# Low halves of the weights: subtraction moved from GpSimd to VectorE, and the order of TensorE's passes

## The reference

```python
for l in range(DEPTH):
    shift, scale, gate = split(silu(c) @ w_ada[l] + b_ada[l], 3)
    proj = (x * (1 + scale) + shift) @ w_in[l]
    y_a = a_b * causal_dwconv(a_c * a_x, conv_a[l]) * silu(a_g)      # width 3
    y_b = dilated_attention(q, k, v, rel_bias) * silu(b_g)           # 8 heads of 64
    y_c = rglru(c_x) * silu(c_g)        # conv of width 4, gates, linear recurrence
    y_d = s5(d_u) * silu(d_g)           # complex diagonal recurrence, gelu, GLU
    y = concatenate([y_a, y_b, y_c, y_d]) @ w_out[l]
    x = layer_norm(ALPHA * x + (1 + gate) * y, ln_g[l], ln_b[l])
```

## Time and profile before

| | |
|---|---|
| Time, median of 3 runs | 2152.26 us (2152.07 to 2152.48) |
| Profiled execution: its span (no other time of it is given) | 2154.4 us |
| Busy: PE, DVE, ACT, POOL | 1850.3, 1515.3, 546.3, 683.6 us |
| Splits on POOL | 256, 629.8 us, mean 2461 ns |
| TensorE clock granted, mean | 0.908 of full speed |

### The profile page before, as it was taken

How to read it: one execution, slowest core, us unless ns; L and a number is a source line. 1 busy time by engine, 2 the same in 40 slices (tenths; PEclk the granted TensorE clock), 3 DMA queues, 4 the chain that set the end, 5 groups by cost and what they waited for, 6 DMA issues and landing times.

```text
span 2154.4 us, 24427 instructions
## 1 busy us (share of the span) xinstructions
PE 1850.3 (86%) x7335; PEld 1366.0 (63%) x7335; DVE 1515.3 (70%) x2383; ACT 546.3 (25%) x796; POOL 683.6 (32%) x341
## 2 busy tenths in 40 slices
PE   2229898899899989969997989998999998979994
PEld 1117566667666766656885756775776775757883
DVE  5787897799789869972324588578668839852755
ACT  2103222322222223222112322322332222232111
POOL 2115232323332232322443523332332333223441
PEclk9558898999899989979998889999998999989997
DMA  7786225524642552353333423421342342234432
GB/s 269 246 288 181 78 80 178 162 82 132 184 126 79 175 161 87 112 161 128 97 98 127 121 74 103 123 90 59 103 130 67 99 121 83 71 100 149 164 98 88
DMA packets 294715, 273.25 MB, mean 127 GB/s; under 512 B 23928, under 2 KB 220896, under 8 KB 291560
## 3 DMA queue, kind: packets, MB, share of 16 engines
q1 hardware_dynamic: 294632, 272.36, 40.3%
HBM read 261.81 MB, written 10.51 MB: 126 GB/s over the span
## 4 chain that ended last, share of the span: by engine, by line
PE 43%; DVE 41%; issue 6%; DMA 6%; SPq 3%; POOL 1%; DVEq 1%; ACT 0%; POOLq 0%
DVE work L1126 13%; PE bank L728 12%; PE bank L729 12%; PE bank L730 12%; DVE ada_acc L1134 7%; DMA ada_in<-in_w_ada 4%; DVE work L1006 3%; DVE work L1005 2%; DVE work L1134 2%; DVE work L1130 2%; DVE y_t L1134 2%; PE bank L869 1%; DVE carry L1134 1%; PE bank L756 1%; DVE carry L1126 1%
## 5 line engine op out<-in xcount | busy, mean ns | idle before, releaser
L484 POOL TENSOR_TENSOR w_lo<-raw,w_hi 128x1024 fp32r<-128x1024 f32 x256 | 629.8, 2461 | 1274.0 <-ACT w_hi L536 1274.0
L728 PE MATMUL bank<-op_hi,w_hi 128*128 128x512 f32 x1536 | 639.8, 417 | 5.1 <-POOL w_lo L484 5.1
L729 PE MATMUL bank<-op_lo,w_hi 128*128 128x512 f32 x1536 | 618.9, 403 | 0.0
L730 PE MATMUL bank<-op_hi,w_lo 128*128 128x512 f32 x1536 | 616.7, 401 | 0.0
L536 ACT ACTIVATE w_hi<-raw 128x1024 fp32r<-128x1024 f32 x256 | 270.8, 1058 | 1178.7 <-PE bank L730 1129.4
L728 PEld LDWEIGHTS bank<-op_hi,w_hi 128*128 128x128 f32 x1536 | 302.6, 197 | 122.6 <-issue 53.2
L730 PEld LDWEIGHTS bank<-op_hi,w_lo 128*128 128x128 f32 x1536 | 300.5, 196 | 67.6
L729 PEld LDWEIGHTS bank<-op_lo,w_hi 128*128 128x128 f32 x1536 | 301.9, 197 | 61.5 <-issue 1.9
L1134 DVE SCALAR_TENSOR_TENSOR ada_acc<-ada_in,cond,ada_acc 128x512 f32<-128x512 f32 (+1 forms) x256 | 258.1, 1008 | 50.8 <-DMA ada_in<-in_w_ada 33.4
L728 PE MATMUL bank<-w_hi,op_hi 128*128 128x512 f32 x512 | 200.0, 391 | 0.0
L729 PE MATMUL bank<-w_lo,op_hi 128*128 128x512 f32 x512 | 199.2, 389 | 0.0
(11 more groups left out here) (188 smaller groups left out, 1747.3 us busy)
## 6 DMA issues: line engine op xcount, KB each, us to landing
raw<-in_w_in SPq DMA_DIRECT2D x192, 512.0 KB, 4.0
ada_in<-in_w_ada SPq DMA_DIRECT2D x256, 256.0 KB, 3.8
raw<-in_w_out SPq DMA_DIRECT2D x64, 512.0 KB, 3.7
raw<-in_w_ada SPq DMA_DIRECT2D x24, 512.0 KB, 5.1
ada_in<-in_w_ada SPq DMA_DIRECT2D x16, 512.0 KB, 5.7
bias_t<-in_w_ada SPq DMA_DIRECT2D x8, 512.0 KB, 5.1
work<-in_w_ada SPq DMA_DIRECT2D x8, 512.0 KB, 6.0
rot<-in_w_ada SPq DMA_DIRECT2D x8, 512.0 KB, 6.1
```

The lines of the kernel that those rows point to most:

```text
L484: pool.tensor_tensor(w_lo[:, n % NHL, :], raw[:, n % NRAW, :], w_hi[:, n % NHL, :].bitcast(F32), ALU.subtract).then_inc(s.lo_done.sem, 1)
L728: pe.matmul(out_, xh, wh, start=first, stop=False)
L729: pe.matmul(out_, xh, wl, start=False, stop=False)
L730: return pe.matmul(out_, xl, wh, start=False, stop=last)
```

## The change

The split of the low halves leaves POOL (L484). `split_lo` becomes a function of DVE, with the same waits, and is called at fixed places of DVE's program (`lo(...)`). PE's piece is taken apart: it waits for hi(n) alone, runs the 16 matmuls that use the weights' high half, waits for lo(n), and runs the other 8. The output stage keeps its order of matmuls. The 15 (layer 0) or 4 ada pieces in one call are divided by lo(21) in layer 0. SP's and ACT's programs are unchanged.

```diff
--- before.py
+++ after.py
@@ -475,31 +475,10 @@
 
 
             for l, s in enumerate(layers):
-                pool.sem_inc(s.lo_done.sem, NRAW)
-                def split_lo(n, step, ahead=0):
-
-                    pool.wait_ge(s.hi_done.sem, s.hi_done.at(n + 1, step) + ahead * HALF)
-
-                    pool.wait_ge(s.mm_done.sem, s.mm_done.at(n + 1 - NHL, step) + ahead * HALF)
-                    pool.tensor_tensor(w_lo[:, n % NHL, :], raw[:, n % NRAW, :],
-                                       w_hi[:, n % NHL, :].bitcast(F32), ALU.subtract).then_inc(s.lo_done.sem, 1)
-
                 for k in range(KT):
-                    if k == FIRST_SPLIT[l]:
-                        split_lo(0, 0)
-                        split_lo(1, 0)
                     pool.wait_ge(s.op_hi.sem, k + 1)
                     pool.tensor_tensor(op_lo[:, k, :], hf[:, k % 2, :], op_hi[:, k, :].bitcast(F32),
                                        ALU.subtract).then_inc(s.op_lo.sem, 1)
-
-
-                with pool.Fori(0, CT) as ct:
-                    for n in range(2, HALF):
-                        split_lo(n, ct)
-                    split_lo(0, ct, 1)
-                    split_lo(1, ct, 1)
-                for n in range(2, W_OUT):
-                    split_lo(n, CT)
 
 
         @block.scalar
@@ -849,14 +828,19 @@
                         u, half = n // 2, n % 2
                         if half == 0:
                             is_free(u % 2, u // 2)
+                        pe.wait_ge(s.hi_done.sem, s.hi_done.at(n + 1, ct))
+                        for j in range(KH):
+                            k, w = half * KH + j, slice(P * j, P * (j + 1))
+                            if u == 0:
+                                pe.wait_ge(s.op_lo.sem, k + 1)
+                            pe.matmul(bank[u % 2][:, :], w_hi[:, n % NHL, w], op_hi[:, k, :], start=k == 0, stop=False)
+                            pe.matmul(bank[u % 2][:, :], w_hi[:, n % NHL, w], op_lo[:, k, :], start=False, stop=False)
+
                         pe.wait_ge(s.lo_done.sem, s.lo_done.at(n + 1, ct))
                         for j in range(KH):
-                            k = half * KH + j
-                            if u == 0:
-                                pe.wait_ge(s.op_lo.sem, k + 1)
-                            w = slice(P * j, P * (j + 1))
-                            mm = product(bank[u % 2][:, :], (w_hi[:, n % NHL, w], w_lo[:, n % NHL, w]),
-                                         (op_hi[:, k, :], op_lo[:, k, :]), k == 0, k == KT - 1)
+                            k, w = half * KH + j, slice(P * j, P * (j + 1))
+                            mm = pe.matmul(bank[u % 2][:, :], w_lo[:, n % NHL, w], op_hi[:, k, :],
+                                           start=False, stop=k == KT - 1)
                         mm.then_inc(s.mm_done.sem, 1)
                         for part in between[n]:
                             part()
@@ -882,6 +866,7 @@
                     c, kk = n // 8, n % 8
                     if n == 8:
                         pe.wait_ge(s.gb.sem, 4)
+                    pe.wait_ge(s.hi_done.sem, s.hi_done.at(n + 1, CT))
                     pe.wait_ge(s.lo_done.sem, s.lo_done.at(n + 1, CT))
                     for t in range(ST):
                         if c >= 2 and kk == 0:
@@ -897,6 +882,13 @@
                             mm.then_inc(s.y_mm.sem, 1)
                     mm.then_inc(s.mm_done.sem, 1)
 
+        def split_lo(dve, s, n, step, ahead=0):
+
+            dve.wait_ge(s.hi_done.sem, s.hi_done.at(n + 1, step) + ahead * HALF)
+            dve.wait_ge(s.mm_done.sem, s.mm_done.at(n + 1 - NHL, step) + ahead * HALF)
+            dve.tensor_tensor(w_lo[:, n % NHL, :], raw[:, n % NRAW, :], w_hi[:, n % NHL, :].bitcast(F32),
+                              ALU.subtract).then_inc(s.lo_done.sem, 1)
+
         def branch_loop(dve, l, s, line, own, tt, ts, stt, repeat):
 
             ADD, SUB, MUL = ALU.add, ALU.subtract, ALU.mult
@@ -909,6 +901,10 @@
                 for b, before in ((1, 5), (4, 1), (5, 1), (6, 1), (7, 1)):
                     s.free[b].local = before
                 pieces = [0]
+
+                def lo(*ns):
+                    for n in ns:
+                        split_lo(dve, s, n, ct)
 
                 def ada(*counts):
 
@@ -950,6 +946,7 @@
                 own(ts(rot[:, 1, :, :], turns, ROUND, ADD, ROUND, SUB), s.own)
                 own(tt(turns, turns, rot[:, 1, :, :], SUB), s.own)
                 own(stt(rot[:, 1, :, :], turns, -1.0, turns, MUL, ALU.max), s.to_act)
+                lo(2)
                 ada(4, 1)
                 for i in range(2):
                     for g in range(2):
@@ -970,7 +967,9 @@
                             own(op_, s.bb_done)
                         else:
                             own(op_, s.own)
+                lo(3)
                 ada(4, 1)
+                lo(4, 5)
 
 
                 unit_copied(dve, s, "c_x", ct)
@@ -979,8 +978,9 @@
                     own(stt(xc, xp[:, k:k + S], col("conv_c", 4 * k), xc, MUL, ADD), s.own)
                 own(stt(xc, xp[:, 0:S], col("conv_c"), xc, MUL, ADD), s.xc_done)
                 ada(4, 2)
-
-                def s5_tile(q):
+                lo(6)
+
+                def s5_tile(q, *splits):
                     cos = rot[:, 1, q, :].unsqueeze(1).to_broadcast([P, 4, TC])
                     sin = rot[:, 0, q, :].unsqueeze(1).to_broadcast([P, 4, TC])
                     w_re, w_im, t_, x_re, x_im = (v.rearrange("p (a b) -> p a b", a=4) for v in s5_s)
@@ -1010,6 +1010,8 @@
                             own(tt(carry[:, 2:3], e_im, cl, MUL), s.own)
                             own(stt(carry[:, 1:2], e_re, cl, carry[:, 0:1], MUL, SUB), s.own)
                             own(stt(carry[:, 3:4], e_re, sl, carry[:, 2:3], MUL, ADD), s.own)
+                        if c == 1:
+                            lo(*splits)
 
                     dve.wait_ge(s.c_done.sem, s.c_done.at(q, ct))
                     own(tt(x_re, w_re, cos, MUL), s.own)
@@ -1044,34 +1046,43 @@
                     unit_copied(dve, s, use_name, ct)
                     return stt(dst, gt[:, i, :], 1.0, gx[:, i, :], ADD, MUL)
 
-                s5_tile(0)
-
+                lo(7)
+                s5_tile(0, 8)
+                lo(9)
 
                 dve.wait_ge(s.from_act.sem, s.from_act.at(2, ct))
                 own(ts(lru_s[0], lru_s[0], 1.0, ADD), s.own)
                 own(dve.reciprocal(lru_s[0], lru_s[0]), s.own)
                 own(tt(lru_s[2], lru_s[2], lru_s[0], MUL), s.own)
+                lo(10)
                 own(ts(lru_s[0], lru_s[0], 2.0, MUL, -1.0, ADD), s.own)
                 own(stt(lru_s[1], lru_s[1], 1.0, xc, ADD, MUL), s.own)
                 own(tt(lru_s[1], lru_s[1], lru_s[2], MUL), s.own)
                 own(dve.tensor_tensor_scan(xc, lru_s[0], lru_s[1], 0.0, MUL, ADD), s.own)
                 ada(3, 1)
-                s5_tile(1)
+                lo(11)
+                s5_tile(1, 12)
+                lo(13)
                 score_max(0, (0, 1))
                 ada(1, 1)
                 score_max(0, (2, 3))
                 ada(4, 1)
+                lo(14)
                 normalise(0)
-                s5_tile(2)
+                s5_tile(2, 15)
+                lo(16)
                 own(silu2(0, "c_g", gx[:, 0, :]), s.own)
 
                 dve.wait_ge(x_io.sem, 16 * (1 + (ST if l else 0)))
                 own(stt(y_out(2), xc, 0.5, gx[:, 0, :], MUL, MUL), s.gate_used[0])
-                s5_tile(3)
+                s5_tile(3, 17)
+                lo(18)
                 ada(2, 1)
                 score_max(1, (0, 1))
+                lo(19)
                 ada(5, 2)
                 score_max(1, (2, 3))
+                lo(20)
                 own(silu2(1, "d_g", silu_d[:, bass.ds(ct, 1), :].rearrange("p o t -> p (o t)")), s.gate_used[1])
                 ada(6, 2)
                 normalise(1)
@@ -1082,7 +1093,9 @@
                 own(tt(s5_s[2], y, y, MUL), s.own)
                 own(ts(s5_s[2], s5_s[2], 0.044715, MUL, 1.0, ADD), s.own)
                 own(tt(gel, s5_s[2], y, MUL), s.to_act)
-                ada(15, 4)
+                ada(7, 4)
+                lo(21)
+                ada(8, 0)
 
                 unit_copied(dve, s, "a_x", ct)
                 v = va[:, 2:2 + S]
@@ -1091,8 +1104,10 @@
                 own(ts(cv, v, col("conv_a", 8), MUL), s.own)
                 own(stt(cv, va[:, 1:1 + S], col("conv_a", 4), cv, MUL, ADD), s.own)
                 own(stt(cv, va[:, 0:S], col("conv_a"), cv, MUL, ADD), s.own)
+                lo(22)
 
                 own(silu2(0, "b_g", gx[:, 0, :]), s.own)
+                lo(23)
                 dve.wait_ge(s.pv_done.sem, s.pv_done.at(2 * ST, ct))
                 own(stt(s5_s[2], bank[7][:, :], 0.5, gx[:, 0, :], MUL, MUL), s.free[7])
                 own(dve.tensor_copy(y_out(1), s5_s[2]), s.gate_used[0])
@@ -1101,6 +1116,8 @@
```

(12 more changed lines are left out.)

## The result

| | before | after |
|---|---|---|
| Time, median (lowest to highest) | 2152.16 us (2150.09 to 2152.48), 4 runs | 2233.91 us (2232.44 to 2236.22), 4 runs |
| Span of the profiled execution | 2154.4 us | 2234.4 us |

The ratio is 1.0385, 95% interval 1.0372 to 1.0398: the change costs 82 us. The forecast was 2189 us (2162 to 2217): the sign was right, the size less than half of what was measured.

The account below looks back on a forecast made before the run. Layer 0 steps were taken as bound by DVE's round, layer 1 steps and the output stage by TensorE. Terms 12 + 7 + 1.6 + 18 = 38.6 us, added to the 2154.4 us span less 2.1, gave 2191, rounded to 2189 (2162 to 2217).

Parts of the forecast that it names:

- The load: DVE's work per step: splits added against collisions returned, -2 us in layer 0 and +2 in layer 1.
- Sum about -8: Layer 0 step, DVE's start to its last 15 ada pieces: about 8 us shorter, returned collisions against added splits and waits.
- lo(14): Layer 0 step, split ahead of normalise(0): must wait for piece 12 and its high half, +4 us.
- The end of the step: Layer 0, after the ada pieces: late lo(21) to lo(23) make PE and DVE wait, +12 us a step.
- Layer 1: Its four steps: PE waits for late lo(0) and lo(2), +7 us in all, bounds 0 to 16.
- The output stage: Layer 1's output stage: PE waits at pieces 10, 18 and 26 behind layer-norm products, +18 us with clock cost.
- The start of layer 0: Layer 0's start: lo(0) comes after the last modulated tile, +1.6 us.
- B: Rival, layer 1's output stage: no waits, since ln_b lands early enough and DVE catches up; 2172 us, chance 0.16.
- C: Rival, end of every layer 0 step: the clock is lost, +10 us a step rather than +3; 2217 us, chance 0.13.
- A: Rival, layer 0 step's end: faster, if DVE's wait for piece 23 is under 9 us; 2143 us, chance 0.12.
- D: Rival, whole kernel: it cancels, load of -2 and +2 and PE's 3.6 us cover swallowing the rest; 2152 us, chance 0.06.
- That order costs nothing: PE's pieces: running 16 high passes first adds no matmuls or weight loads and gives 3.6 us before lo(n) is needed.

Follow-up runs that it names:

- Experiment 1: Kernel after with only SP's queue edited: layer 0's ada loads behind raw(6) and raw(7), and two behind raw(21), issued one weight piece earlier; 2208.11 us.
- experiment 10: Kernel after with ada loads moved, lo splits re-placed in steps and layer 1's output stage, and lo(14) behind normalise(0); 2088.84 us, ratio 0.9709.
- Experiment 2: Kernel after with layer 0's lo(21) moved ahead of normalise(1), lo(22) and lo(23) between the 15 ada pieces; 2192.09 us, ratio 1.0181.
- Experiment 6: Kernel after with lo(2) alone moved ahead of DVE's wait for the step's small loads; 2214.48 us, ratio 1.0285.
- Experiment 3: Kernel after, layer 1's output stage only: lo(10) ahead of the layer-norm products, lo(18) and lo(26) after the sixth, following splits between mixed tiles; 2218.8 us.
- experiment 7: Kernel after with the edits of Experiment 1 and Experiment 2 together; 2165.08 us, ratio 1.0058.
- experiment 4: Kernel before, splits still on GpSimd, with only PE's order changed to 16 high passes, then 8 low ones; 2151.85 us, ratio 0.9984.
- experiment 5: Kernel after with PE's old matmul order in the branch loop, so a piece waits for lo(n) at its start; 2294.81 us, ratio 1.0654.
- experiment 11: experiment 10 plus useless GpSimd work, six 128x160 subtractions for each of pieces 2 to 23 of a branch step; 2154.55 us, ratio 1.0015.
- experiment 12: experiment 4 (splits on GpSimd, high passes first) with each branch-step split cut into six short subtractions; 2079.51 us, ratio 0.9652.

## Why the prediction was right and wrong

**The load, right.** Forecast: -2 us of DVE's load in a layer 0 step and +2 in one of layer 1; measured -6.2 and -2.8. A split takes 1.24 us (1.22 to 1.28 given, 1.28 taken). Without its 24 splits (29.7 us) a step of layer 0 has 155.6 - 29.7 = 125.9 us of DVE work where it had 161.8: 35.9 returned (forecast 33); layer 1 132.0 - 29.7 = 102.3 from 134.8: 32.5 (forecast 29). So neither a split nor the collisions are the reason for the loss.

**Layer 0's section from DVE's start to its last 15 ada pieces: this is the step that failed.** The prediction said "Sum about -8" (157.6 to 149.6); measured is 973.20 - 813.22 = 160.0, +2.4. Its work is as forecast: 31.6 us of collisions returned (31), 23.2 of splits (24.3), and the wait for s5_drive gone (6.4 for 5.6). What failed is the wait for ada loads, which the sum put at nothing: it rose by 8.4 us, from 2.0 to 10.4. All items of the sum were about DVE, ACT and PE; none followed the semaphore that a late lo(n) also feeds: raw(n+3) waits for it, SP's queue is in order, and the ada loads stand behind raw(n+3). The bounds name the ada loads, but only as something that could cost nothing. Experiment 1 moved only these loads and returned 7.5 of the 10.4 us. Most of the rest is lo(14), which I had at +4 with everything and whose wait alone was 4.3 to 5.1 (experiment 10 shows that moving it is worth some 3 us a step), and idle times of about 0.2 us ahead of the other splits. Over the four steps layer 0 missed by 43.9 us: DVE waits 31.4 us more for ada loads, and experiment 1 returned 26.6. Of the other items that the traces show, the first step's late start is the largest (7.3 us later against piece 0, where the forecast had +1.6 at the layer's start); it was not tested. The working had the queue before it: it counted the wait of bias_t's loads, and not those of w_ada.

**The end of the step, right.** E, the end of the 15 ada pieces, is 988.75; the step ends at 1013.6: E+24.9, where E+26 was forecast and before had E+14. PE's waits were to be 10 and 4 us and are 11.53 and 3.31; DVE's wait at the product that reads bank 7 was to be near 8 and is 10.12. The slow clock behind the two waits cost 1.8 and 1.7 us, more than the 1 to 2 in all of the sum. Experiment 2 took the whole back: 11 us a step.

**Layer 1, right in size by luck.** +6.3 for 7, and PE's wait before piece 2's low passes is there, 4.0 to 4.8 us (forecast 4.7). But 5.5 of the 6.3 us are in the first step, which was to cost about 0 (with the layer's start, 2.8 us shorter, it is 2.7), and the other three, at 1.7 each and 2 behind the last, grew by 0.9 in all: the wait for lo(0) was to be 1.8 us and is 0.5, and DVE's start moved by 0.3 to 1.1 us, not 2. Experiment 6 took the wait in piece 2 away.

**The output stage, right.** +20.1 for 18, with waits of 7.0, 3.2 and 3.2 us at the pieces named, and 6.9 us in place of 4.6 for the slower matmuls behind them. Experiment 3 took them away. The start of layer 0, +1.6 by forecast, was 0.7 shorter up to piece 0; what the late lo(1) costs shows behind it.

**The rivals.** B (the output stage doesn't wait) is refuted by the three waits and experiment 3. C (+10 a step from a lost clock) had nearly the size, but not the mechanism: the granted clock of the step is 0.93, where it was 0.92. A named the right place, and its own condition, a wait for piece 23 under 9 us, was missed by little (10.12): with the end repaired and the loads as well (experiment 7) layer 0 is 16.3 us faster than before, not 36. D (it cancels) is refuted by the 82 us. That the split on DVE as such is bad is refuted by experiment 10: same instructions, same counts, 145 us faster than the change as made.

**The order of the passes.** "That order costs nothing" holds (experiment 4), and its cover of 3.6 us a piece is worth some 60 us here (experiment 5).

A point of the Trainium skill that the prediction leaned on, an exclusive lock on a port pair shared by DVE and GpSimd, held for a whole instruction (SBUF — State Buffer, § SBUF: two separate sides), is in agreement with the runs: the stretched durations left with the splits and came back in part with useless work (experiment 11). What the runs add are prices: 1.24 us of DVE for a whole split, and about half of that for one cut into six, at more busy time of GpSimd.

Open: why a short GpSimd instruction costs DVE less was not taken apart; other widths than 160 and 172 columns were not run, nor short splits in the output stages, nor short splits with TensorE's old order, nor experiment 12 with moved loads, though DVE waits 51.5 us for ada loads in it.

## What to carry to other kernels

When a producer moves to an in-order engine, follow its semaphore to every waiter, not only to the consumer that one has in mind: the ring's next load waits for it, and whatever stands behind that load in its queue. A move that is even in busy time is decided by where each instruction stands: the same 256 splits gave 2233.9 and, placed anew and with a few loads moved, 2088.8 us, and the cheap test is to place each ahead of the engine's next long wait and behind work that it needn't hold up. Before moving work off an engine that disturbs another, try cutting its instructions short: here that needed no new order on DVE (TensorE's high passes stood first), and gave the most.

## What the runs showed of the hardware

| | whole splits on GpSimd | none | useless work, 128x160 | splits of 128x172 |
|---|---|---|---|---|
| kernel | before | experiment 10 | experiment 11 | experiment 12 |
| one subtraction on GpSimd, median | 2.40 us | - | 0.51 us | 0.56 us |
| GpSimd busy, all | 683.6 us | 56.1 | 772.4 | 979.4 |
| DVE busy, without its own splits | 1515.3 us | 1196.5 | 1272.6 | 1391.0 |
| one ada accumulation on DVE, mean | 990 ns | 752 | 791 | 811 |

A 128x1024 subtraction on GpSimd took DVE 1.24 us on the mean; six of 128x160, which take 6 x 0.51 = 3.1 us together by their median, took 0.5 (88.9 us over 176 groups, DVE's own splits included). I had taken the loss as a property of the load on GpSimd and not of its granularity. The last column still has the 64 whole splits of the output stages in it; at 1.24 us for each of these, a split cut into six comes to (1391.0 - 1196.5 - 64 x 1.24) / 192 = 0.6 us, an estimate. DVE's products of the same width that read one operand from PSUM took 691 ns before and 690 to 691 in the three experiments.
